# Token shift and the third head group's preparation in the merged projection stage, modulation in the chunk chain

## The chip, the core and the metric

The kernel runs on one core of a Trainium2 chip, as one launch. The metric is the device time of that launch in microseconds (us). TensorE, VectorE, ScalarE, GpSimd and SyncE run their own instruction streams and wait for each other on semaphores. In profile rows they are PE (with PEld for its weight loads), DVE, ACT, POOL and SP. All data is float32.

## The reference, cut to what matters

One diffusion step of a two-layer trunk over 640 tokens (128 of a prompt, 512 of a sample), width 1024. In each layer the modulated input h is multiplied by `w_in` into three groups of columns, each for one kind of token mixer: latent attention (8 heads), a gated linear recurrence "hgrn" (4 heads, two directions), and a delta-rule recurrence "rwkv" (4 heads, two directions), which is the third head group. Then follow an output projection with layernorm, an expert-choice layer and a second layernorm.

```python
cols = h @ p['w_in']
mla_cols, hg_cols, rw_cols = _split(cols, (MLA_COLS, HG_COLS, RW_COLS))
...
def _token_shift(a, mu):
    prev = jnp.pad(a[:, :-1], ((0, 0), (1, 0), (0, 0)))
    nxt = jnp.pad(a[:, 1:], ((0, 0), (0, 1), (0, 0)))
    return a + mu[0] * (prev - a) + mu[1] * (nxt - a)
...
feat = _token_shift(cols, mu)
r, k, v, wd_f, wd_b, ad_f, ad_b, gd = _split(feat, ...)
gate = jax.nn.sigmoid(gd) @ g2
kk = heads(k * k_k)
kk = kk * lax.rsqrt(jnp.maximum(jnp.sum(kk * kk, -1, keepdims=True), 1e-12))
for d, (wd, ad) in enumerate(((wd_f, ad_f), (wd_b, ad_b))):
    w_log = -jnp.exp(-jax.nn.softplus(-(w0[d] + jnp.tanh(wd) @ w2[d])) - 0.5)
    aa = jax.nn.sigmoid(a0[d] + ad @ a2[d])
    kd = heads(k * (1.0 + (aa - 1.0) * k_a))
    ... # recurrence over tokens, forward and backward
```

The modulation `silu(c) @ ada_w + ada_b` gives six vectors for each layer. Four of them (shift, scale and gates for what comes after the mixers) are needed only behind the mixers.

## The kernel before

Each layer is a row of phases, and a phase ends with a barrier of all engines. The phases that matter here are `phase_mix`, `phase_attention`, `phase_rwkv` and `phase_output`; the x tile, 5 x 1024 columns, is kept in its own memory, nearly everything else shares one arena.

**Merged projection stage (`phase_mix`).** h is transposed, and the projections are made in groups, each into one PSUM bank. A unit is one tile of 128 tokens in one direction of the hgrn recurrence, ten units in all, in an order written out by hand (`units`). For each unit TensorE makes the score products (`scores`, L712 and L722), a transposition (L739), one *item* of projection (`item`: two groups of eight matmuls), the output of the unit before (`out`, L755 to L769) and a state product (L779). The items are 5 of attention columns (m, lines L692 and L696), 2 of gates (g) and 9 of rwkv columns (r, both L684). Items alternate between banks 0 and 1; ScalarE evacuates each (`evacuate`, L850 for r). VectorE in each unit masks the scores (L1032), then makes half of the factors of a unit two ahead if the direction is forward (`run_levels`, 22 steps, L578 to L592) and the other half in the unit behind it (up to L611), then takes the output of the unit before (`collect`, L975 and L977) and updates the state (`state`, L994). GpSimd makes the factors of the backward units. After unit 9 come four more r items, the norm products of hgrn, and VectorE's reciprocals (L1059). rwkv columns lie in `rwT` with zero columns as padding.

**Attention (`phase_attention`).** 8 heads x 5 tiles of queries, software-pipelined over TensorE, VectorE and ScalarE. L1355 is the first rope operation of each head. Beside it GpSimd makes the token shift: for each of 9 rwkv chunks six scalings (L1318) and two additions (L1321, L1322). The x tile is loaded again here.

**rwkv (`phase_rwkv`).** First the preparation: tanh and squares on ScalarE (L1540, L1543), norm products (L1705), 16 low-rank products (`lora`, L1714), sigmoids out of them (L1552), reciprocals (L1906), the gate product (L1719), transpositions of v (L1726, L1729), then for each of four (direction, pair) a cumulative decay (L1920) with its exponentials and factors on VectorE, ScalarE and GpSimd (L1914 to L1937, L1573 to L1575, L1634 to L1646). Between these TensorE makes the four late vectors of the modulation (`modulate(s)`, L1691 and L1696) from 16 pieces of `ada_w`, 1 MB each, through four slots. L1965 is VectorE's first operation of the next part, in which 25 steps invert triangular blocks (L1758 to L1800). The last part is the chunk chain: ten steps, each with two chunks, that pass a state on: state products (L1839, L1844, twice), a copy by VectorE, a product with the inverse (L1861), the matrices of the next step (L1825, L1830), and the state update by VectorE (L2005, L2010). Normalisation and two rounds of transpositions end the phase (L1887).

**Output (`phase_output`).** The output projection (L2169) and the first layernorm, which reads the x tile.

## Time and profile before

| what | value |
|---|---|
| median of 3 runs | 3010.34 us (3006.26 to 3012.44) |
| the profiled execution's own time | 3006.61 us |
| its span, first to last instruction | 3004.8 us |
| PE busy | 2613.5 us (87%) |
| DVE, ACT, POOL busy | 1129.8, 467.5, 761.0 us |
| mean granted TensorE clock | 0.944 of full speed |

In a row, names are those of the program, L is the line, x is the number of instructions. A float32 matmul shows as two PE records. "Idle" is the time for which the engine stood still just before the row, with what ended it. The clock column gives the granted clock as a share of 2.4 GHz: 1.00 is the upper level, 0.50 the lower one, and what lies between is a mean over the stretch.

### The profile page before, as it was taken

Reading aid. Unit: us, or ns where it says so; the run is one execution under the profiler, and the core shown is the slowest. Engines: PE = TensorE matmul, PEld = TensorE weight load, DVE = VectorE, ACT = ScalarE, POOL = GpSimd, SP = SyncE. Lnnn points to the kernel's source line nnn. Section 1 sums busy time; section 2 is a strip of 40 time slices with the busy share of each in tenths; the row PEclk is TensorE's granted clock in tenths of the full one; section 3 lists DMA queues with packets and bytes.
Section 4 is the critical chain, followed back from the end, with each engine's and each line's share of the span. In section 5 each row is a group of like instructions: output and inputs, shape, how many; then the busy total and the mean of one; then the engine's idle time right before and its main releaser. Section 6 shows DMA issues by size and latency. Waiting matters only on the chain. (4 is left out here: it accounts for less than half of the span.)

```text
span 3004.8 us, 72192 instructions
## 1 busy us (share of the span) xinstructions
PE 2613.5 (87%) x32434; PEld 1773.8 (59%) x32434; DVE 1129.8 (38%) x2438; ACT 467.5 (16%) x992; POOL 761.0 (25%) x892
## 2 busy tenths in 40 slices
PE   6999888887675999999889997888977669999994
PEld 3677455467444666666446764553864456666662
DVE  3464356755433111111154724668453321111113
ACT  2100233421110000000031013334211100000001
POOL 1253092343041000000052522903421300000002
PEclk9999899999886999999999999999998789999997
DMA  7010200410345999999730102006005369999984
GB/s 282 15 38 29 76 1 1 182 53 30 120 166 189 387 398 387 397 396 402 293 138 16 43 22 76 1 1 232 4 29 212 141 235 395 395 397 390 398 351 140
DMA packets 76874, 560.56 MB, mean 187 GB/s; under 512 B 14056, under 2 KB 16168, under 8 KB 37656
## 3 DMA queue, kind: packets, MB, share of 16 engines
q1 hardware_dynamic: 70424, 534.97, 44.8%
q0 software_dynamic: 6144, 20.98, 3.1%
q8 instruction: 257, 4.21, 0.6%
q14 instruction: 49, 0.40, 0.0%
HBM read 528.78 MB, written 27.13 MB: 185 GB/s over the span
## 5 line engine op out<-in xcount | busy, mean ns | idle before, releaser
L2473 PEld LDWEIGHTS ps<-arena 128*64 128x64 f32 x16384 | 579.0, 138 | 89.7 <-issue 87.1
L2473 PE MATMUL ps<-arena 128*64 128x80 f32 x16384 | 599.4, 234 | 14.0 <-issue 9.4
L2487 PE MATMUL ps<-arena 128*80 128x512 f32 x1024 | 466.7, 600 | 0.0
L2548 DVE TENSOR_TENSOR arena<-arena,ps 128x160 f32<-128x160 f32 x128 | 41.1, 321 | 721.3 <-ACT arena L2508 721.3
L2487 PEld LDWEIGHTS ps<-arena 128*80 128x80 f32 x1024 | 143.7, 149 | 229.8 <-issue 218.9
L2508 ACT ACTIVATE arena<-ps 128x160 f32<-128x160 f32 x128 | 38.9, 304 | 1007.6 <-PE ps L2473 1007.6
L2234 POOL DMA_INDIRECT sum_d<-arena x32 | 45.6, 1427 | 583.6 <-DVE arena L2540 583.6
L2228 POOL DMA_INDIRECT arena<-h_d,arena x32 | 40.2, 1256 | 499.0 <-DVEq L2523 431.3
L684 PE MATMUL ps<-arena,x_sb 128*128 128x128 f32 (+1 forms) x576 | 158.5, 434 | 0.0
L684 PE MATMUL ps<-arena 128*128 128x512 f32 (+1 forms) x512 | 139.9, 434 | 4.5 <-ACT arena L833 4.5
L2169 PE MATMUL ps<-arena 128*128 128x512 f32 x320 | 141.9, 606 | 2.1 <-PEq L1502 2.1
L684 PEld LDWEIGHTS ps<-arena,x_sb 128*128 128x128 f32 x576 | 88.0, 191 | 69.1 <-issue 68.9
L684 PEld LDWEIGHTS ps<-arena 128*128 128x128 f32 x512 | 77.7, 191 | 65.3 <-issue 60.3
L2169 PEld LDWEIGHTS ps<-arena 128*128 128x128 f32 x320 | 62.0, 195 | 81.1 <-issue 81.1
L1364 DVE TENSOR_REDUCE arena<-ps 128x1 f32<-128x768 f32 (+1 forms) x80 | 65.8, 822 | 95.4 <-PE ps L1199 88.9
L1657 POOL TENSOR_TENSOR arena<-arena,rwl_sb 128x512 f32<-128x512 f32 x50 | 63.7, 1280 | 103.1 <-ACT arena L1587 56.2
L2540 DVE SCALAR_TENSOR_TENSOR arena<-ps,arena 80x512 f32<-80x512 f32 x64 | 45.0, 742 | 112.4 <-PE ps L2487 112.4
L1287 ACT ACTIVATE arena<-ps,arena 128x768 f32<-128x768 f32 (+1 forms) x80 | 63.6, 795 | 134.9 <-DVE arena L1365 112.8
L1032 DVE TENSOR_TENSOR arena<-ps,arena 128x512 f32<-128x512 f32 (+1 forms) x100 | 60.7, 634 | 61.8 <-PE ps L712 59.0
L1318 POOL TENSOR_SCALAR arena<-arena,pcol_sb 128x128 f32<-128x128 f32 x72 | 79.9, 1127 | 0.0
L1133 PE MATMUL ps<-arena 128*128 128x512 f32 (+1 forms) x192 | 59.0, 443 | 23.3 <-DVE arena L1355 23.3
L1212 PE MATMUL ps<-arena 128*64 128x64 f32 x1600 | 64.2, 226 | 16.0 <-DVE arena L1390 15.8
(352 smaller groups left out, 3856.8 us busy)
## 6 DMA issues: line engine op xcount, KB each, us to landing
arena<-in_ex_w SPq DMA_DIRECT2D x128, 2048.0 KB, 15.2
arena<-in_ex_w SPq DMA_DIRECT2D x128, 1024.0 KB, 13.4
arena<-in_ada_w SPq DMA_DIRECT2D x32, 1024.0 KB, 8.0
arena<-in_ada_w SPq DMA_DIRECT2D x8, 2048.0 KB, 16.3
x_sb<-in_w_t SPq DMA_DIRECT2D x18, 512.0 KB, 3.4
arena<-in_w_t SPq DMA_DIRECT2D x16, 512.0 KB, 6.2
x_sb<-in_x SPq DMA_DIRECT2D x2, 2560.0 KB, 18.3
h_d<-x_sb SPq DMA_DIRECT2D x10, 512.0 KB, 2.6
```

What stands on the lines that cost most here:

```text
L684: i = nc.tensor.matmul(dst[:, 0:c1 - c0], w[:, k, :], e.hT[:, k, c0:c1], start=k == 0, stop=k == KD - 1)
L1032: nc.vector.tensor_tensor(am[:, u % 2, at].rearrange("p (b n) -> p b n", b=rep), src.rearrange("p (b n) -> p b n", b=rep), hgf[:, dr:dr + ...
L1133: i = nc.tensor.matmul(ps[:, 7, 0:c1 - c0], uq[:, k, h * P:(h + 1) * P], cqT[:, k, c0:c1], start=k == 0, stop=k == 2)
L1212: m = nc.tensor.matmul(ps[c * C:(c + 1) * C, 6, (i % 2) * DV:(i % 2 + 1) * DV], pT[:, i % 2, k * P + c * C:k * P + (c + 1) * C], V[:, c0 / ...
L1287: nc.scalar.activation(pr[:, i % 2, 0:c1 - c0], sc[:, 0:c1 - c0], ACT.Exp, bias=negm[:, i:i + 1], scale=SCALE, accum_out=rsum[:, i:i + 1]) ...
L1318: c.add(nc.gpsimd.tensor_scalar(shifted[:, 1 + by, c0:c1], e.rwT[:, n, q0:q0 + c1 - c0], scale[:, n:n + 1], None, ALU.mult))
L1364: v.link(nc.vector.reduce_max(negm[:, i:i + 1], sc[:, 0:c1 - c0], AX))
L1657: nc.gpsimd.tensor_tensor(Mj[:, n % 4], raw[:, t], e.rwl[:, :, j + 2:j + 3, :].to_broadcast([P, 2, HH, C]), ALU.mult).then_inc(S["mj"], 1)
L2169: m = nc.tensor.matmul(ps[:, 2 * (t % 4) + n, :], e.mixT[:, k, t * P:(t + 1) * P], half, start=k == 0, stop=k == KD - 1)
L2234: e.nc.gpsimd.indirect_dma_start(e.sum_d, bass.IndirectOffsetOnAxis(ap=mem["iu"][:, x:x + 1], axis=0), mem["yR"][:, x % 2, :], None, compu ...
L2473: m = nc.tensor.matmul(gated(j)[c * 64:(c + 1) * 64, f, a, :], w13[q % WG][:, a, k, f * P + c * 64:f * P + (c + 1) * 64], xT[:, x % 2, k, ...
L2487: m = nc.tensor.matmul(rows_out(x, h), he[:, x % 2, f, :], w2[:, q % WP, f % 2, h * 512:(h + 1) * 512], start=f == 0, stop=f == KD - 1)
```

## The change

- **Token shift.** Each r item is evacuated by ScalarE with the scale 1 - mu0 - mu1 (`om`), and VectorE then adds mu0 times the token before and mu1 times the token after straight from the item's PSUM bank: four operations (`shift`). The bank is free only after the last of them. The padding and the GpSimd work in attention go.
- **Order of the items.** g and r items come first, the five m items last, behind unit 9. r items follow in the order 6, 7, 2, 3, 0, 1, 8, 4, 5. All their weights go through a ring of five slots in the x tile.
- **Preparation.** Tanh, squares, norm products (two new items n, each two matmuls with an evacuation by VectorE), square roots and the reciprocals (`norms`) are made in units 3 to 9. Behind unit 9 come the 16 `lora` products through four banks, then the m items; beside these run the sigmoids, decays, exponentials and factors (`lora_out`, `exponents`, `keys`, `scaled`, `decays`, `factors`). Their results stay in memory through attention: `KB` at the arena's end, `AR` in the x tile.
- **Modulation.** `modulate(i)` handles one piece, and two pieces are put in each step of the chunk chain: one behind the first round of state products, one at the step's end. The slots are three.
- **Loads.** The x tile is loaded again after the last step of the chunk chain. The first half of `w_out` is loaded behind the last piece of `ada_w`. Attention's weights lie elsewhere. `phase_mix` has more semaphores, which SyncE clears at the start of attention.

The diff, cut to its core:

```diff
@@ phase_mix: the items and their banks
-    groups += [("m", t, s) for t in range(TILES) for s in range(2)]
-    groups += [("g", c, s) for c in range(2) for s in (1, 0)]
-    groups += [("r", c, s) for c in range(NRW) for s in (1, 0)]
+    gates, shifts_a, shifts_b, shifts_c = (0, 1), (6, 7, 2, 3, 0), (1,), (8, 4, 5)
+    items = [("g", c) for c in gates] + [("r", c) for c in shifts_a] + [("n", p) for p in range(2)]
+    items += [("r", c) for c in shifts_b + shifts_c] + [("m", t) for t in range(TILES)]
...
+    served = [[("g", 0)], [("g", 1), ("r", 6)], [("r", 7)], [("r", 2)], [("r", 3)], [("r", 0)],
+              [("n", 0), ("n", 1), ("r", 1)], [("r", 8)], [("r", 4)], [("r", 5)]]
...
-        return n % 8 if n < NX else n % 2
+        return n % 8 if n < NX else n % 2 if kind != "m" else ((0, 1), (6, 7), (0, 1), (2, 3), (4, 5))[a][s]
@@ phase_mix, TensorE
             for u in range(1, U):
                 scores(u)
                 if units[u] not in last:
                     turn(u)
-                item(u + (u > 1))
+                for i in served[u][:1] if u == 1 else served[u]:
+                    item(*i)
                 out(u - 1)
                 if units[u] not in last:
                     chunk_state(u)
                 if u == 1:
-                    item(2)
-            item(11)
+                    item(*served[u][1])
             out(U - 1)
-            item(12)
-            item(13)
+            for n, (w, dr, pair, i) in enumerate(lora):
+                if n >= 4:
+                    pe.wait_ge(S["lo_ev"], n - 3)
+                nc.tensor.matmul(ps[:, lora_bank[n % 4], 0:c1 - c0], wwa[...], F[:, 6 + w, c0:c1], ...)
+            item("m", 0)
             ...
@@ phase_mix, VectorE
+            def shift(kind, c):
+                ...
+                dve.wait_ge(S["rw_om"], 2 * k + 2)
+                for i in range(2):
+                    v.add(nc.vector.scalar_tensor_tensor(F[:, c, c0 + 1:c1], ps[...], col("mu0", c), F[:, c, c0 + 1:c1], ALU.mult, ALU.add))
+                v.join()
+                for i in range(2):
+                    nc.vector.scalar_tensor_tensor(F[:, c, c0:c1 - 1], ps[...], col("mu1", c), ...).then_inc(S["pj_dve"], 1)
...
+                if u in (7, 8):
+                    norms(u - 7)
...
                 if dr == 0 and u + 2 < U:
                     nxt = run_levels(u + 2)
                     ...
+                for kind, i in served[u]:
+                    if kind != "g":
+                        shift(kind, i)
                 if u:
                     collect(u - 1)
@@ phase_attention
-            sp.dma_start(e.x[:, :, :], (e.x_d if l else d["x"])...).then_inc(S["ld_xr"], 16)
...
-            for n in range(NRW):
-                for by, scale in ((0, om), (-1, mu[0]), (1, mu[1])):
-                    ...
@@ phase_rwkv, TensorE
                 with_state(2, chunks, 0, s, S["rh_ps"])
+                if 0 <= 2 * s - 1 < ADA_PIECES:
+                    modulate(2 * s - 1)
                 pe.wait_ge(S["rh_sb"], s + 1)
...
                 with_state(3, chunks, 1, s, S["y_ps"])
+                if 2 * s < ADA_PIECES:
+                    modulate(2 * s)
@@ phase_rwkv, SyncE
             sp.wait_ge(S["rw_fin"], 1)
+            sp.wait_ge(S["y_ps"], 2 * NS)
+            sp.dma_start(e.x[:, :, :], (e.x_d if l else d["x"])...).then_inc(S["ld_xr"], 16)
```

## Rows read from the trace of the kernel before

**Rows 1.** Stretches: width, busy us (instructions) of PE, PEld, DVE, ACT, POOL, clock, DMA:

```profile
40.80:338.70 297.90, 293.98 (x1904) 200.97 (x1904) 148.93 (x370) 47.29 (x91) 107.93 (x236) 0.99 0.13 47
338.70:545.00 206.30, 171.51 (x1390) 105.57 (x1390) 113.14 (x253) 68.39 (x162) 88.43 (x75) 0.95 0.08 29
545.00:616.50 71.50, 58.48 (x245) 21.07 (x245) 56.48 (x64) 34.48 (x60) 25.08 (x16) 0.90 0.63 243
616.50:706.00 89.50, 78.77 (x2580) 76.75 (x2580) 45.24 (x75) 19.17 (x38) 41.78 (x36) 0.94 0.04 9
706.00:803.60 97.60, 61.35 (x915) 54.49 (x915) 56.31 (x106) 17.18 (x37) 21.79 (x28) 0.86 0.05 20
2027.00:2095.40 68.40, 55.70 (x244) 20.02 (x244) 56.47 (x64) 34.22 (x59) 25.09 (x16) 0.95 0.66 254
```

**Rows 2.** Timeline, units 6 and 7: start, duration, engine, line [idle before]:

```profile
228.76 8.82 PE L684 MATMUL ps<-arena,x_sb 128*128 128x512 f32 x32
...
237.04 0.29 DVE L584 TENSOR_TENSOR arena<-arena 128x128 f32<-128x128 f32 x1
...
240.67 0.42 DVE L977 COPY arena<-ps 128x256 f32<-128x256 f32 x1 [3.33 <-PE ps L769]
...
242.43 1.97 DVE L1032 TENSOR_TENSOR arena<-ps,arena 128x512 f32<-128x512 f32 x3 [0.21 <-DVE arena L994]
...
254.87 0.42 DVE L611 TENSOR_TENSOR arena<-arena 128x256 f32<-128x256 f32 x1
...
256.98 0.42 DVE L975 TENSOR_TENSOR arena<-arena,ps 128x256 f32<-128x256 f32 x1 [1.68 <-PE ps L769]
```

**Rows 3.** Groups by line, whole span: busy us, mean ns of one:

```profile
L1059 DVE RECIPROCAL arena<-arena 128x640 f32<-128x640 f32 x4 | 16.6, 4153 | 34.8 <-ACT arena L908 34.8
```

**Rows 4.** Attention: line L1318 (ns, first and last start), and timeline of VectorE:

```profile
L1318 POOL TENSOR_SCALAR arena<-arena,pcol_sb x36: 599/1336/1809, 380.1 to 462.1; 128x128 f32<-128x128 f32 x18, 128x512 f32<-128x512 f32 x18
...
408.75 0.70 DVE L1355 TENSOR_TENSOR arena<-ps,rope_sb 32x512 f32<-32x512 f32 x1
...
429.22 0.70 DVE L1355 TENSOR_TENSOR arena<-ps,rope_sb 32x512 f32<-32x512 f32 x1
...
511.04 0.70 DVE L1355 TENSOR_TENSOR arena<-ps,rope_sb 32x512 f32<-32x512 f32 x1
```

**Rows 5.** Timeline, rwkv preparation:

```profile
566.48 2.40 PE L1719 MATMUL ps<-arena 128*128 128x256 f32 x10 [2.72 <-ACT arena L1554]
...
573.92 1.22 ACT L1561 ACTIVATE arena<-ps 128x1280 f32<-128x1280 f32 x1
...
591.26 3.25 PE L1738 MATMUL ps<-blk_sb,arena 128*128 128x2 f32 x20
...
618.68 0.75 DVE L1965 TENSOR_TENSOR arena<-ps,rwl_sb 128x256 f32<-128x256 f32 x2 [0.50 <-PE ps L1758]
```

**Rows 6.** Timeline of TensorE: one modulation piece, and waits in the chunk chain:

```profile
586.00 1.89 PE L1691 MATMUL ps<-arena,scT 128*2 128x512 f32 x8 [0.61 <-DMA arena<-in_ada_w]
...
733.82 0.70 PE L1839 MATMUL ps<-arena 128*64 128x128 f32 x4 [4.49 <-DVEq L2016]
...
754.06 0.68 PE L1861 MATMUL ps<-arena 64*64 64x64 f32 x16 [0.55 <-DVE arena L2001]
...
759.79 0.44 PE L1839 MATMUL ps<-arena 128*64 128x128 f32 x4 [1.42 <-DVEq L2016]
```

**Rows 7.** Timeline, state update beside and without GpSimd's constants:

```profile
727.93 2.91 POOL L1678 TENSOR_TENSOR arena<-arena 128x1280 f32<-128x1280 f32 x1
...
729.49 4.22 DVE L2010 TENSOR_TENSOR arena<-arena 128x256 f32<-128x256 f32 x2 [0.47 <-PE ps L1844]
...
751.12 1.16 DVE L2010 TENSOR_TENSOR arena<-arena 128x256 f32<-128x256 f32 x2 [0.48 <-PE ps L1844]
```

**Rows 8.** Timeline, end of the rwkv phase:

```profile
800.23 2.39 PE L1887 MATMUL ps<-ident_sb,arena 128*128 128x128 f32 x10 [12.50 <-DVEq L2042]
```

**Rows 9.** DMA issues: count, KB each, median us to landing:

```profile
x_sb<-in_x SPq DMA_DIRECT2D x2, 2560.0 KB, 18.3
```

More of the change, by code:

```diff
@@ L53 @@
 SCALE = float(QK) ** -0.5
-PAD = NTOK + 3
 TOKC = MLA_COLS + HH * HD
@@ L634, in _, with ring_load @@
             sp.wait_ge(S["pj_ps"], NX)
-            sp.dma_start(w_m1, d["w_m1"][l]).then_inc(S["ld_m1"], 16)
-            sp.dma_start(w_m2a, d["w_m2"][l, :, 0:6]).then_inc(S["ld_m2"], 16)
-            sp.wait_ge(S["pj_ps"], NH)
-            for c in range(2):
-                sp.dma_start(gw[c], d["w_t"][l, HGT + c]).then_inc(S[f"ld_gw{c}"], 16)
+            def ring_load(i):
+                kind, c = ring[i]
+                if i >= WRING:
+                    sp.wait_ge(S["pj_ps"], begins[ring[i - WRING]] + 2)
+                slot, _, w = weights(kind, c)
+                sp.dma_start(w, d["w_t"][l, HGT + c + 2 * (kind == "r")]).then_inc(S[f"ld_wt{slot}"], 16)
+            for i in range(WRING + 2):
+                ring_load(i)
             sp.wait_ge(S["hg_state"], 2)
@@ L658, in project @@
                 kind, a, s = groups[n]
-                if n < NX:
-                    if n >= 8:
-                        evacuated(pe, n - 8)
-                elif n == NX:
+                before = [m for m in range(n) if pbank(m) == pbank(n)]
+                if before:
+                    evacuated(pe, before[-1])
+                if n == NX:
                     for m in range(NX - 2, NX):
                         evacuated(pe, m)
-                elif n > NX + 1:
-                    evacuated(pe, n - 2)
                 dst = ps[:, pbank(n), :]
@@ L795, in _ @@
                 evacuated(pe, m)
-            item(0)
+            for i in served[0]:
+                item(*i)
             for u in range(1, U):
@@ L892, in _ @@
                 evacuate(n)
-            item(0)
+            for i in served[0]:
+                item(*i)
             for u in range(1, U):
@@ L909, in _ @@
                                      bias=e.eps[:, 0:1], scale=1.0 / HD).then_inc(S["hg_rt"], 1)
-            item(14)
-            item(15)
+            exponents(2)
+            item("m", 1)
+            exponents(3)
+            for t in range(2, TILES):
+                item("m", t)
             e.done("act", a)
@@ L1437, in phase_rwkv @@
     So, z1 = e.part(z1, 4, P)
-    assert z1 <= e.a1
+    assert z1 <= e.a0 + 2560
     X, z1 = e.part(e.a1, TILES, 2, HH, C)
-    assert z1 <= e.a1 + 4 * PAD
+    assert z1 <= e.a1 + 4 * NTOK
     ys, z1 = e.part(e.a1, TILES, HH * HD)
-    assert z1 <= e.a1 + 4 * PAD
-    ada = [e.part(late + n * 2048, 2, 2, 512)[0] for n in range(ADA_SLOTS)]
-    assert late + ADA_SLOTS * 2048 <= z
-    above = e.a2 + 4 * NCH * 2 * C + 4 * 2 * NTOK
+    assert z1 <= e.a1 + 4 * NTOK
+    ada = []
+    for _ in range(ADA_SLOTS):
+        v, z = e.part(z, 2, 2, 512); ada.append(v)
+    above = e.a2
     arow = e.part(above, 4, 512)[0]
     abias = e.part(above + 4 * 512, 512)[0]
-    mid, z = e.part(z, 4, NCH)
-    end, z = e.part(z, 4, NCH)
-    G, z = e.part(z, 4, NCH)
     Gb, z = e.part(z, 4, NCH, 2)
@@ L1518, in _ @@
                              ).then_inc(S[f"ld_ap{i % ADA_SLOTS}"], 16)
+            sp.wait_ge(S["ap_ps"], ADA_PIECES)
+            k = 0
+            for dst in first_half(e):
+                n = dst.shape[1]
+                sp.dma_start(dst, d["w_out"][l, :, 0, k:k + n, :]).then_inc(S["ld_wo0"], 16)
+                k += n
             sp.wait_ge(S["ap_row"], 8)
@@ L1716, in _, with modulate @@
-            pe.wait_ge(S["lo_ev"], len(lora))
-            pe.wait_ge(S["rw_sg"], 1)
+            def modulate(i):
+                s = i // 4
+                if i == 0:
+                    pe.wait_ge(S["ld_ab"], 16)
+                if i % 4 == 0 and s >= 2:
+                    pe.wait_ge(S["ap_row"], 2 * (s - 1))
+                pe.wait_ge(S[f"ld_ap{i % ADA_SLOTS}"], 16 * (i // ADA_SLOTS + 1))
+                for k in range(2):
+                    for c in range(2):
+                        m = nc.tensor.matmul(gate_sums(s)[c], e.scT[:, 2 * (i % 4) + k, :], ada[i % ADA_SLOTS][:, c, k, :],
+                                             start=i % 4 == 0 and k == 0, stop=False, skip_group_check=True)
+                m.then_inc(S["ap_ps"], 1)
+                if i % 4 == 3:
+                    for c in range(2):
+                        r = C + 2 * s + c
+                        m = nc.tensor.matmul(gate_sums(s)[c], e.ident[C:C + 8, r:r + 1].to_broadcast([8, 2]), abias[C:C + 8],
+                                             start=False, stop=True, skip_group_check=True)
+                    m.then_inc(S["ap_sum"], 1)
```

506 lines of the change are left out of this document (263 added, 243 removed).

## The prediction

> **What bounds the kernel now.** I read the table of stretches first, since the change moves work between stages with different limits. In layer 0 the merged stage takes 297.90 us and TensorE is busy for 293.98 of them, at a granted clock of 0.99: TensorE sets its pace. In attention no engine is near full (TensorE 171.51 of 206.30 us), and GpSimd's 88.43 us lie beside the others. In the preparation of rwkv (71.50 us) TensorE has 58.48, VectorE 56.48, ScalarE 34.48; chains of products and elementwise work set it, and the clock is 0.90. The inverse takes 89.50 us at 0.94, the chunk chain with its tail 97.60 at 0.86 with TensorE busy for 61.35 [rows 1]. Then I read the timeline where the new work is to go. The collections of units 6 and 7 begin 16.3 us apart (240.67 and 256.98), and in unit 6, whose item starts at 228.76, VectorE, done with its factor steps at 237.33, stands idle 3.33 us before it collects; in unit 7 it ends its factors at 255.29 and stands idle 1.68 [rows 2]. So an even unit has some 3.3 us of room on VectorE and an odd one some 1.7 or less.
>
> The profiled execution took 3006.61 us, 1.8 more than its span, and 3.7 less than the median of 3010.34. I make the sum as a difference and put it on the median.
>
> **Merged stage.** A shift is four operations of VectorE that read PSUM, two of 512 columns and two of 128. The nearest row is a 512-column operation with PSUM input at 0.70 us [rows 4]; with 0.35 for the narrow ones, which is my choice (half; no row has it), that is 2.1 us. Bounds are 1.4 (overlapped) and 4.2 (double). A shift delays the collection behind it, and with it the state and the next mask.
> - Units 2, 4, 8, 9 have 3.3 us of room: 0.
> - Units 3 and 5 have about 1.5: +0.6 each, +1.2.
> - Unit 1 has two items, and the second one's ring slot and shift stand behind the state product: shift, collection, state and mask take 2.1, 0.4, 0.9 and 2.0 us (the mask 1.97 [rows 2]), 5.4 in all, against 2.4 of work of TensorE beside them: +3.0.
> - Unit 6 has both norm products and item r1. Only two banks alternate, so the second norm product needs the first one's bank evacuated by VectorE, which has issued its 22 factor steps ahead of it. These end at 237.33 [rows 2]. Then 0.7 of evacuation, the product, and again an evacuation before r1: r1 starts at 240.0 instead of 228.76. That is +11.2.
> - In unit 7 `norms` puts a reciprocal of 4.15 us [rows 3] ahead of the factor steps, and a shift of 2.1 behind them, of which 1.68 is room; with 0.5 for the multiplication, +5.1. Unit 8 has the same reciprocal but even unit's room and no factor steps of the same length: 0.
> - The 16 `lora` products behind unit 9 take 8 pairs of 1.10 (8.82/8, the rate of an item [rows 2]) = 8.8 if nothing holds them, and 13.2 if ScalarE's sigmoids, through four banks, set the pace. I take 10.9. The m items that follow give cover for all that VectorE, ScalarE and GpSimd still do: TensorE has about 10.9 + 9.6 + 2.8 + 4 x 9.6 = 61.7 us there, VectorE about 46, GpSimd 41 to 53. So the tail costs 0 with 9 to 15 us of room.
> - Clock. Where TensorE has stood still for long, the rows behind show it slow: the same state product takes 0.70 us after 4.49 of idle, 0.44 otherwise [rows 6]. The stage has 0.99 now. I expect the 8.3 us of idle in unit 6 to bring such a stretch of some 7 us, 3.6 lost, and as much in sum in the other places: +7.0; bounds 0 and 14.
>
> Sum: 1.2 + 3.0 + 11.2 + 5.1 + 10.9 + 7.0 = +38.4 per layer.
>
> **Attention.** GpSimd's scalings run from 380.1 to 462.1; a head that has them beside it takes 20.47 us (408.75 to 429.22), and the next four (429.22 to 511.04), two of them without, 20.46 each [rows 4]. Taking them away gives 0. Sixteen more semaphores are cleared by SyncE before the loads: +0.7.
>
> By the Trainium skill, "SBUF — State Buffer", section "SBUF: two separate sides", GpSimd and VectorE hold a shared pair of ports one at a time, so that without GpSimd's scalings VectorE should run freer; the head's 20.47 and 20.46 us do not agree that it costs time here, and the sum would be lower by what the heads gained.
>
> **Preparation.** Now 73.7 us from 545.00 [rows 1] to L1965 at 618.68 [rows 5]. What stays: start and loads that land 3.9 us in, the gate product with the transpositions and the last evacuation (566.48 to 573.92 + 1.22 = 8.7 [rows 5]), at the lower clock some 4.5 more, the bonus product (3.25 at 591.26 [rows 5]; I take 2.8), 3.3 of last copies and the start 0.5: 23.7. That is -50.0. In layer 1 the stage is 68.40 long, 3 less [rows 1]: -47.1. Bounds: 17 and 31 us remaining.
>
> **Modulation in the chain.** A chain step is set by the state's way through TensorE and VectorE. A piece behind the first state products takes 1.89 [rows 6] and lies where TensorE waits 0.55 for VectorE's copy [rows 6]; 1.34 is added to the path, 8 times, 10.7. A piece at the step's end lies beside a wait of 1.42 [rows 6]: 0.5 added, 6 times (two are covered otherwise), 3.0. Four bias rows at 0.5: 2.0. The slow clock of the chain (0.86 [rows 1]) is partly won back by a busier TensorE, -3.7. Together +12. Bounds +2 (all in gaps that rows show larger at the start, 4.49 [rows 6]) and +24 (all 16 pieces on the path with their bias rows). The weights' ring of three slots is a DMA of 1 MB per step and has time: 0.
>
> **Loads.** The x tile is issued when the last y product is done, about 787.2, and first read behind the wait of 12.50 us for the normalisation, which ends at 800.23 [rows 8]; the load of 2560 KB took 18.3 us median to landing [rows 9], beside attention's weights. Alone I estimate 10 us and so 0; at 18.3 it would cost 4.8 per layer. `w_out` and the other moved loads have 2 to 3 us of room at least: 0, and 3 if not.
>
> **Sum.** Layer 0: 38.4 + 0.7 - 50.0 + 12 = +1.1. Layer 1: 38.4 + 0.7 - 47.1 + 12 = +4.0. Both: +5.1, and 3010.3 + 5.1 = 3015.4; I say 3015.5.
>
> **Rivals.**
> *A, the forecast:* the moved work costs on TensorE's path what it saved. Its own range 3004 to 3027. Chance 0.40.
> *B, the clock (the other side):* a stage of 0.90, one of 0.94 and one of 0.86 [rows 1] lie behind one another. If the 0.99 of the merged stage stays in spite of unit 6, and the shorter preparation and the fuller chain let the clock stay up, the 7.0 of loss go, and of the 4.7 + 8.6 us that the low clock costs the inverse and the chain now (78.77 x 0.06 and 61.35 x 0.14) I let half, 6.7, come back: 13.7 per layer, minus 27 in all, near 2988. It decides for faster from 5.6 us per layer. For it: TensorE loses many of its waits. Against it: unit 6's stall is as long as the ones behind which rows show it slow. Chance 0.25.
> *C, the shift on VectorE:* the 2.1 us (4.2 at the upper bound) come through in every unit, because VectorE's room exists in no unit once its steps are late, and the clock does not recover before unit 8: 8 x 0.7 more of shift and 5.5 of clock, +11 per layer, near 3038. For it: VectorE has 148.93 us busy in the stage [rows 1], in bursts before TensorE's waits. Chance 0.20.
> *D, GpSimd and VectorE in the tail:* the state update took 4.22 us beside GpSimd's 2.91 us addition, and 1.16 without it [rows 7]. If the two engines' 35 to 47 and 41 us behind unit 9 go one after the other, they need 76 to 88 against 61.7 of TensorE: +14 per layer at the lower end, near 3043. Against it: most of VectorE's operations there are narrow or have PSUM or one input, and 88.43 us of GpSimd slowed no head in attention [rows 1, 4]. Chance 0.08.
>
> The exclusive lock of the Trainium skill, "SBUF — State Buffer", section "SBUF: two separate sides", is the reason why this could go so for operations with two SBUF inputs; on the state update the trace agrees with it.
>
> *E, the x load:* it lands late, +4.8 per layer, near 3025. Chance 0.07.
>
> **How the numbers follow.** About 0.2% (6 us) is what a measurement of this kernel can tell from no change. Faster means below 3004.3: nearly all of B (0.24) and 0.07 of A, 0.31. Same, up to 3016.4: about 0.19 of A, the rest of B and 0.02 of E, 0.22. Slower: 0.14 of A, C, D and the rest of E, 0.47. A range that leaves out 2 in 10 goes from under B's 2988 to over D's 3043: 2984 to 3046, as the cases have both signs.
>
> **What would show it.** In the merged stage an idle of over 7 us of TensorE ahead of r1 in unit 6, and one of 4 to 5 in unit 7; a stage longer by 35 to 42 us; heads of 20.5 us; L1965 some 23 us into the rwkv phase; chain steps that grow by 1.3 to 1.8 us where they hold pieces; no wait for the x tile. Wrong it would be if unit 6's stall were short, if the granted clock of inverse and chain rose to 0.98 or more, or if VectorE's row of the tail ended behind the last m item.

## The result: 0.6% faster, where no change was forecast

The changed kernel takes 2991.65 us (median of 5 runs, 2987.45 upward), the kernel before 3009.07 in the same measurement; the ratio is 0.994, with a 95% interval of 0.9924 to 0.9956. The forecast was 3015.5, a little over no change. The time lies in the range, 2984 to 3046, but on the other side of the kernel before than the forecast did, 24 us from it. One of the five runs took 3296 us and was disturbed; the median of the other four is 2990.2 us, and the ratio leaves it out.

The profiled execution of the changed kernel has a span of 2989.5 us against 3004.8. Both spans can be divided at the same operations: the first projection, attention's first transposition, the first product of the inverse, the first matrix product of the chunk chain, the transposition of its final state, the first product of the output projection. Differences of such starts, in us:

| stretch | layer 0 before | after | difference | layer 1 before | after | difference |
|---|---|---|---|---|---|---|
| first projection to attention | 295.91 | 324.77 | +28.86 | 295.91 | 325.09 | +29.18 |
| attention and rwkv preparation | 270.36 | 221.32 | -49.04 | 267.03 | 219.91 | -47.12 |
| inverse | 87.10 | 87.34 | +0.24 | 87.86 | 90.59 | +2.73 |
| chunk chain | 83.28 | 92.48 | +9.20 | 81.33 | 92.50 | +11.17 |
| tail up to the output projection | 16.79 | 16.79 | 0.00 | 16.86 | 16.80 | -0.06 |

With the 0.71 us ahead of the first projection and -0.50 and -0.6 behind the output projections these make -15.3. The forecast had +39.1, -50.0 (-47.1), 0 and +12 for them. Three of the four are right to a few us. The first is 10 us too high in each layer, 20 of the 24 us of the miss.

Here are the stretches of the changed kernel in layer 0, as in [rows 1]: the last m items with all the elementwise work beside them, what is left of the preparation, the inverse, the chain.

```profile
318.50:366.10 47.60, 47.56 (x170) 27.22 (x168) 42.58 (x30) 19.00 (x32) 39.20 (x22) 1.00 0.00 1
577.10:597.00 19.90, 12.53 (x60) 10.48 (x60) 1.94 (x8) 5.41 (x13) 0.00 (x0) 0.74 0.48 173
597.00:684.40 87.40, 76.91 (x2562) 75.21 (x2562) 44.26 (x71) 18.56 (x37) 42.64 (x36) 0.94 0.02 4
684.40:776.90 92.50, 86.42 (x1065) 53.26 (x1065) 45.73 (x97) 17.17 (x38) 22.83 (x28) 1.00 0.50 172
```

The preparation is 19.90 us long where it was 71.50 [rows 1]. The chain has become a stretch of TensorE, 86.42 of 92.50 us at the upper level of the clock. The row of [rows 1] for the chain, with its 0.86, also holds the wait for the normalisation at its end. Between the same two operations as in the last row above, the kernel before had 0.92:

```profile
703.60:786.90 83.30, 59.87 (x921) 53.35 (x921) 46.51 (x97) 12.48 (x30) 21.79 (x28) 0.92 0.07 27
```

 In the first row of the changed kernel TensorE has no gap at all: what VectorE, ScalarE and GpSimd do there is hidden.

The timeline of the changed kernel's TensorE, and two rows of VectorE, through units 6 to 8 and behind unit 9:

```profile
229.16 1.25 PE L731 MATMUL ps<-arena,blk_sb 128*128 128x512 f32 x4
...
237.91 2.50 PE L731 MATMUL ps<-arena,blk_sb 128*128 128x512 f32 x4 [7.50 <-DVE arena L1152]
...
240.76 9.41 PE L727 MATMUL ps<-arena,x_sb 128*128 128x512 f32 x32 [0.36 <-DVE arena L1152]
...
271.22 0.70 PE L769 MATMUL ps<-arena 128*128 128x256 f32 x2 [1.48 <-DVEq L1112]
...
275.72 1.60 PE L759 MATMUL ps<-arena 128*128 128x128 f32 x12 [1.58 <-DVE arena L1236]
...
307.98 7.02 PE L864 MATMUL ps<-arena 128*128 128x512 f32 x24
...
316.26 2.43 PE L864 MATMUL ps<-arena 128*128 128x512 f32 x8 [1.26 <-ACT arena L958]
```

```profile
237.17 0.88 DVE L1152 TENSOR_SCALAR arena<-ps 128x512 f32<-128x512 f32 x2
...
258.14 4.14 DVE L1170 RECIPROCAL arena<-arena 128x640 f32<-128x640 f32 x1
```

The stall of unit 6 is where it was forecast: TensorE stands for 7.50 us until VectorE, behind its factor steps, evacuates the first norm products at 237.17. The item behind it starts at 240.76, forecast 240.0. But it runs in 9.41 us, nearly the 8.82 of [rows 2]. The clock is at its lower level for 6.8 us, from 235.0 to 241.8, and TensorE is at work in only 3.53 of them: the rest is stall (columns as in [rows 1]).

```profile
233.00:234.00 1.00, 0.00 (x0) 0.00 (x0) 0.96 (x4) 0.00 (x0) 0.84 (x3) 1.00 0.00 0
235.00:241.80 6.80, 3.53 (x6) 1.69 (x7) 3.81 (x13) 0.00 (x0) 0.23 (x1) 0.50 0.01 2
242.00:243.00 1.00, 1.00 (x3) 0.38 (x2) 0.00 (x0) 0.00 (x0) 0.00 (x0) 1.00 0.00 0
```

The intervals between the starts of two units' score products, read from the same timelines (us; layer 1 agrees to 0.05 except where noted):

| unit | 0 | 1 | 2 | 3 | 4 | 5 | 6 | 7 | 8 |
|---|---|---|---|---|---|---|---|---|---|
| before | 28.71 | 24.94 | 15.80 | 16.70 | 16.30 | 16.31 | 16.31 | 16.30 | 15.86 |
| after | 28.27 | 24.17 | 17.10 | 16.31 | 16.31 | 16.30 | 28.51 | 17.86 | 17.70 |

An m item takes some 0.4 us longer than an r or g item, so the units that lost m items (0, 1 with two, 2 and 3) are shorter by that, and the tail behind unit 9 longer. In unit 2 the interval grew by 1.3 us in spite of it; the wait there is 1.7.

### The profile page after: what moved, and what is told of

The parts are those of the page before. It is cut to its first block and busy times, and to the rows that moved or that the text cites. A ratio compares the mean times of both kernels' runs of the same rounds, so it can differ in the third digit from the quotient of the medians.

```text
span 2989.5 us, 72116 instructions
## 1 busy us (share of the span) xinstructions
PE 2615.2 (87%) x32434; PEld 1776.5 (59%) x32434; DVE 1151.2 (39%) x2486; ACT 477.8 (16%) x1000; POOL 614.1 (21%) x754
## 5 line engine op out<-in xcount | busy, mean ns | idle before, releaser
L2549 PEld LDWEIGHTS ps<-arena 128*64 128x64 f32 x16384 | 579.7, 138 | 87.0 <-issue 84.3
L2549 PE MATMUL ps<-arena 128*64 128x80 f32 x16384 | 600.2, 234 | 11.2 <-issue 6.6
L727 PE MATMUL ps<-arena,x_sb 128*128 128x512 f32 (+1 forms) x704 | 195.5, 436 | 2.3 <-ACT arena L916 1.6
L727 PEld LDWEIGHTS ps<-arena,x_sb 128*128 128x128 f32 x704 | 108.4, 192 | 88.5 <-issue 84.7
L2245 PEld LDWEIGHTS ps<-arena 128*128 128x128 f32 x320 | 62.6, 196 | 81.6 <-issue 81.4
L727 PE MATMUL ps<-arena 128*128 128x128 f32 (+1 forms) x384 | 104.6, 434 | 4.3 <-DVE arena L1213 4.3
L727 PEld LDWEIGHTS ps<-arena 128*128 128x128 f32 x384 | 58.1, 191 | 49.8 <-issue 45.0
L1359 PE MATMUL ps<-arena 128*128 128x512 f32 (+1 forms) x192 | 59.6, 447 | 23.4 <-DVE arena L1565 23.4
L1438 PEld LDWEIGHTS ps<-arena 128*64 128x64 f32 x1600 | 53.3, 138 | 41.1 <-DVE arena L1600 26.4
L1422 PE MATMUL ps<-arena 96*128 96x512 f32 (+1 forms) x160 | 74.6, 547 | 2.5 <-ACT arena L1500 2.5
```

The costliest lines, as they stand in the source:

```text
L727: i = nc.tensor.matmul(dst[:, 0:c1 - c0], w[:, k, :], e.hT[:, k, c0:c1], start=k == 0, stop=k == KD - 1)
L1359: i = nc.tensor.matmul(ps[:, 7, 0:c1 - c0], uq[:, k, h * P:(h + 1) * P], cqT[:, k, c0:c1], start=k == 0, stop=k == 2)
L1422: m = nc.tensor.matmul(ps[:, 2 * (i % 2), 0:min(512, c1 - c0)], QT[:, h % 2, t * P:(t + 1) * P], Kh[:, h % 2, c0:min(c0 + 512, c1)], start ...
L1438: m = nc.tensor.matmul(ps[c * C:(c + 1) * C, 6, (i % 2) * DV:(i % 2 + 1) * DV], pT[:, i % 2, k * P + c * C:k * P + (c + 1) * C], V[:, c0 / ...
L2245: m = nc.tensor.matmul(ps[:, 2 * (t % 4) + n, :], e.mixT[:, k, t * P:(t + 1) * P], half, start=k == 0, stop=k == KD - 1)
L2549: m = nc.tensor.matmul(gated(j)[c * 64:(c + 1) * 64, f, a, :], w13[q % WG][:, a, k, f * P + c * 64:f * P + (c + 1) * 64], xT[:, x % 2, k, ...
```

## The experiments

All twelve kernels are edits of the changed kernel; 3, 8 and 12 join several. Each was timed beside the kernel before, whose median lay between 3007.5 and 3009.4 us. Differences below are against the changed kernel's 2991.65. Its own interval is 0.9924 to 0.9956, and those of 2, 4, 7 and 11 overlap it; what these four show rests on the intervals of units, which repeat to some 0.01 us, and not on their medians.

**1. The norm products evacuated first.** In VectorE's loop over units:

```diff
+                for kind, i in served[u]:
+                    if kind == "n":
+                        shift(kind, i)
                 if dr == 0 and u + 2 < U:
                     nxt = run_levels(u + 2)
...
-                    if kind != "g":
+                    if kind == "r":
                         shift(kind, i)
```

> Unit 6: VectorE evacuates the two norm products ahead of its 22 factor steps instead of behind them. Theory 1 (the stall is VectorE's order, and the lower clock behind it is small): the waits of 7.50 and 0.36 us go, and with them the 1.25 + 0.59 us by which the second norm products and the item behind the stall ran slower; 9 to 10 us per layer, 18 to 20 in all, some 2973 us. Theory 2 (the forecast's clock term of 7.0 us per layer is real and hangs on this stall): 14 us per layer and more, under 2965. Theory 3 (the stall only moves, to the factor steps that come 3 us later): less than 4 us per layer, over 2984.

Measured: 2970.13 us, ratio 0.9871 (0.9856 to 0.9887), 21.5 us less. TensorE in unit 6:

```profile
229.17 1.25 PE L731 MATMUL ps<-arena,blk_sb 128*128 128x512 f32 x4
...
230.98 1.35 PE L731 MATMUL ps<-arena,blk_sb 128*128 128x512 f32 x4 [0.56 <-DVE arena L1152]
```

The wait of 7.50 is one of 0.56 and the unit takes 20.12 us in both layers instead of 28.5: 8.4 each, 16.8 in all. Theory 1 stands for the stall. The remaining 4.7 us of the medians are not in any unit; where the profiled executions differ besides is told below.

**2. Both reciprocals in unit 8.**

```diff
-                if u in (7, 8):
-                    norms(u - 7)
+                if u == 8:
+                    for p in range(2):
+                        norms(p)
```

> Both reciprocals (4.14 us each) in unit 8, where VectorE has no factor steps, instead of one in unit 7 and one in unit 8. Theory 1 (in unit 7 the reciprocal delays the factors that unit 8's scores wait for): unit 7 goes from 17.86 to 16.3 us and unit 8 from 17.70 to 15.9, 3.4 per layer, 6.8 in all, some 2985 us. Theory 2 (the two together push unit 8's shift and collection): the gain of unit 7 comes back as a wait in unit 8, within 2 us of 2991.6.

Measured: 2984.71 us, ratio 0.9916 (0.9899 to 0.9933), 6.9 less. Unit 7 takes 16.31 us and unit 8 15.85, in both layers: theory 1, to the tenth. Unit 8's scores wait for unit 8's factors, and these stood behind the reciprocal in unit 7; in unit 8 there are no factors left to make. The wait for the masks in unit 8 goes too, with the token shift as wide as before.

**3. Both edits together.**

> The edits of the two kernels before together. If both waits are independent: 26 us in all less than the changed kernel, some 2965 to 2967 us, with TensorE's granted clock at 1.00 through units 2 to 9. If VectorE's lateness is one and the same in units 6 to 8: no more than the first edit alone, some 2973.

Measured: 2964.76 us, ratio 0.9852 (0.9837 to 0.9866), 26.9 less. The two waits are independent. Units 6, 7 and 8 take 20.13, 16.30 and 15.86 us. The same stretch of unit 6, first in the changed kernel, then in this one:

```profile
224.80:253.40 28.60, 20.74 (x156) 14.10 (x151) 15.40 (x42) 3.99 (x5) 9.19 (x21) 0.88 0.00 1
```

```profile
222.90:243.10 20.20, 19.07 (x160) 13.43 (x157) 14.71 (x42) 2.93 (x6) 10.93 (x26) 1.00 0.00 1
```

TensorE is busy for 20.74 and 19.07 us: the lower clock made its work 1.7 us longer, no more, though the mean clock of the stretch was 0.88.

**4. A narrow token shift.** Both additions of a shift work on 8 columns of each block:

```diff
-   v.add(nc.vector.scalar_tensor_tensor(F[:, c, c0 + 1:c1], ps[:, pbank(n + i), 0:c1 - c0 - 1], col("mu0", c), ...))
+   v.add(nc.vector.scalar_tensor_tensor(F[:, c, c0 + 1:c0 + 9], ps[:, pbank(n + i), 0:8], col("mu0", c), ...))
...
-   nc.vector.scalar_tensor_tensor(F[:, c, c0:c1 - 1], ps[:, pbank(n + i), 1:c1 - c0], col("mu1", c), ...)
+   nc.vector.scalar_tensor_tensor(F[:, c, c0:c0 + 8], ps[:, pbank(n + i), 1:9], col("mu1", c), ...)
```

> The token shift works on 8 columns of each block only (the rest is left out), with the same four instructions and semaphores. Theory 1 (VectorE's room covers the shift nearly everywhere): the waits of 1.43 us in unit 2 and 1.58 in unit 8 go, about 3 us per layer, 6 in all, some 2985 us. The forecast's terms for it (3.0 + 1.2 + 1.7 per layer): 12 in all, 2980. The rival in which the shift comes through in every unit (2.1 us each, nine units, two layers): 30 and more, under 2962.

Measured: 2986.6 us, ratio 0.9925 (0.9908 to 0.9941), 5.1 less. Unit 2 takes 15.81 us (17.10) and unit 8 16.41 (17.70): 2.6 us per layer, 5.2 in all. Units 3 to 5 and 7 are as they were. The shift costs nothing there; its width costs 1.3 us in each of two units. In unit 8 that holds only as long as the reciprocal stands in unit 7: kernel 2 has the whole shift and no wait there, so the two gains don't add.

**5. A double token shift.** The four operations are issued twice, with the item's bank given back after the last (each neighbour is then added twice).

> The token shift's four operations are issued twice (each neighbour is added twice), 2.1 us more of VectorE behind each rwkv item, with the item's bank held longer. Theory 1 (even units have 3.3 us of room and the shift uses 2.1 of it, odd units less): the waits come out at 1 to 2 us in most units, 6 to 12 us per layer, 12 to 24 in all, 3004 to 3016 us. The rival of no room anywhere: 2.1 x 9 x 2 = 38 us, 3029. Full cover: 0.

Measured: 3022.53 us, ratio 1.0041 (1.0029 to 1.0053), 30.9 more, above what theory 1 gave and below the 38 of the rival. The units 2 to 8 take 20.87, 18.26, 18.21, 17.47, 29.74, 19.02, 21.44 us: 3.8, 2.0, 1.9, 1.2, 1.2, 1.2 and 3.7 more, 14.9 in sum per layer. In units 3 and 4 TensorE waits in the middle of the scores for VectorE's masks:

```profile
184.38 1.60 PE L759 MATMUL ps<-arena 128*128 128x128 f32 x12 [1.68 <-DVE arena L1246]
...
202.60 1.60 PE L759 MATMUL ps<-arena 128*128 128x128 f32 x12 [1.64 <-DVE arena L1246]
```

So the cover is real but thin: in units 3 to 7 the first shift is free (kernel 4), and of the 2.0 us of the second more than half is paid, in even and odd units alike. Units 2 and 8 grow by more than the work that was added; the items behind their waits take 10.20 and 9.51 us instead of 8.82, so part of it is the clock. The rival without any room, 38 us, is near for the second shift and wrong for the first.

**6. Thin modulation in the chain.** Each piece multiplies 32 of 512 columns (the others are left out); loads, waits and the bias rows stay.

```diff
-   m = nc.tensor.matmul(gate_sums(s)[c], ..., ada[i % ADA_SLOTS][:, c, k, :], ...)
+   m = nc.tensor.matmul(gate_sums(s)[c][:, 0:32], ..., ada[i % ADA_SLOTS][:, c, k, 0:32], ...)
```

> The modulation's pieces in the chain work on 32 of 512 columns (the other columns are left out), with the same loads and waits; the bias rows stay. Theory 1 (TensorE is now the chain's limit, so that the pieces cost what does not fit in the 1.97 us of waits of a step): the chain goes from 92.5 us back to 83 to 85, 16 to 19 in all, some 2974 us. Theory 2 (the fuller chain wins back clock, 3.7 us per layer as forecast): the chain without pieces falls to a clock of 0.92 to 0.94 and takes 86 to 88, 9 to 13 in all, some 2981 us.

Measured: 2975.05 us, ratio 0.9887 (0.9865 to 0.9908), 16.6 less. The chain takes 85.49 and 85.23 us, 7.1 less per layer, 14.3 in all. Its stretches in the two layers:

```profile
682.50:768.00 85.50, 69.09 (x1065) 57.22 (x1065) 44.28 (x97) 17.17 (x38) 22.80 (x28) 0.90 0.53 186
2147.10:2232.30 85.20, 67.37 (x1064) 56.53 (x1064) 45.79 (x97) 17.17 (x38) 22.81 (x28) 0.92 0.54 187
```

Without the full pieces the clock falls from 1.00 to 0.90 and 0.92, as theory 2 says (it gave 0.92 to 0.94) and theory 1 leaves out. The length of the chain lies between the two, and the time, 2975, is the one that theory 1 gave. The full pieces bring some 17 to 18 us of TensorE's time into the chain (86.4 less 69.1, and 85.5 less 67.4), and the chain gets 7 longer. The two parts of that can be seen in the sums by line over the chain of layer 0, for the kernel before, the changed kernel and this one (busy us, mean ns, idle us before with what ended it). First the state products, the product with the inverse and the matrices before the change:

```profile
L1839 PE MATMUL ps<-arena 128*64 128x128 f32 x160 | 17.4, 297 | 17.2 <-DVEq L2016 16.1 <-DVE arena L1995 1.0
...
L1825 PE MATMUL ps<-arena 64*128 64x128 f32 x160 | 13.4, 313 | 0.9 <-DVE arena L1980 0.9
...
L1861 PE MATMUL ps<-arena 64*64 64x64 f32 x160 | 7.7, 242 | 5.5 <-DVE arena L2001 5.5
```

The same and the pieces and bias rows in the changed kernel:

```profile
L1835 PE MATMUL ps<-arena,scT 128*2 128x512 f32 x128 | 30.2, 592 | 0.0
L1960 PE MATMUL ps<-arena,x_sb 128*64 128x128 f32 x160 | 16.6, 286 | 4.2 <-DVEq L2092 3.2 <-DVE arena L2071 1.0
...
L1946 PE MATMUL ps<-x_sb,arena 64*128 64x128 f32 x160 | 11.6, 284 | 0.9 <-DVE arena L2057 0.9
...
L1984 PE MATMUL ps<-arena 64*64 64x64 f32 x160 | 6.8, 224 | 1.1 <-DVE arena L2077 1.1
...
L1841 PE MATMUL ps<-arena,ident_sb 8*2 8x512 f32 x16 | 4.1, 586 | 0.0
```

And two of them with thin pieces:

```profile
L1960 PE MATMUL ps<-arena,x_sb 128*64 128x128 f32 x160 | 16.6, 286 | 13.2 <-DVEq L2092 12.2 <-DVE arena L2071 1.0
...
L1946 PE MATMUL ps<-x_sb,arena 64*128 64x128 f32 x160 | 15.3, 346 | 0.9 <-DVE arena L2057 0.9
```

The pieces fill 17.3 us of waits (16.1 to 3.2, and 5.5 to 1.1), and the matrices, the same products, take 11.6 us instead of 13.4, or of 15.3 with thin pieces.

**7. TensorE busy in unit 6's stall.** The second product of the first norm item is issued 13 times.

```diff
+                    for _ in range(13 if (a, s) == (0, 0) else 1):
                         i = nc.tensor.matmul(dst[:, 0:c1 - c0], e.blk[:, :], rn[:, a, c0:c1], start=True, stop=True)
```

> The second product of the first norm item is issued 13 times instead of once (its result is the same), so that TensorE is at work through most of the 7.50 us for which it stood in unit 6; VectorE's order stays that of the changed kernel. If the low clock behind the stall costs the 1.84 us that the rows behind it show (2.50 against 1.25, 9.41 against 8.82): unit 6 goes from 28.5 to some 26.7 us, 2 to 4 us in all, some 2988 us. If the forecast's clock term were right (3.6 us behind this stall, 7.0 per layer): 24.9 us or less, 7 to 14 in all, 2978 to 2985.

Measured: 2988.9 us, ratio 0.9935 (0.9922 to 0.9949); not to be told from the changed kernel. The repeated products took less time than I had given them and left a wait of 4.81 us, behind which TensorE was slow again (10.65 us for the item in layer 0). Unit 6 took 29.73 and 28.28 us, the first longer than in the changed kernel. The clock was at its lower level for 6.8 us again, but it fell at the end of the shorter stall, and TensorE was at work in nearly all of them:

```profile
236.40:243.20 6.80, 5.96 (x8) 2.68 (x9) 1.52 (x4) 0.00 (x0) 0.00 (x0) 0.50 0.00 0
```

A wait that is only shortened need not give the clock back, and kernel 11 fills all of it.

**8. One norm item a unit.** Norm items behind the r items of units 6 and 7, both reciprocals in unit 8, square roots at the end of unit 7.

```diff
-              [("n", 0), ("n", 1), ("r", 1)], [("r", 8)], [("r", 4)], [("r", 5)]]
+              [("r", 1), ("n", 0)], [("r", 8), ("n", 1)], [("r", 4)], [("r", 5)]]
```

> One norm item behind the rwkv item of unit 6, the other behind that of unit 7, and both reciprocals in unit 8; nothing then waits for an evacuation of norm products. Against the kernel with both orders changed (unit 6 20.12 us): unit 6 and 7 each 16.3 + 0.7 us, so 2.4 us per layer less, some 2960 us. If the square roots come too late for the reciprocals in unit 8: unit 8 grows from 15.9 by what unit 6 gives back, 2965.

Measured: 2977.17 us, ratio 0.9891 (0.9876 to 0.9906): faster than the changed kernel but 12 us slower than 3. Both branches of what I expected were wrong. Units 6 and 7 take 21.45 and 23.48 us, unit 8 15.85.

```profile
240.60 1.51 PE L731 MATMUL ps<-arena,blk_sb 128*128 128x512 f32 x4 [2.29 <-DVE arena L1164]
...
262.80 2.50 PE L731 MATMUL ps<-arena,blk_sb 128*128 128x512 f32 x4 [3.04 <-DVE arena L1164]
```

The norm product needs the bank that the r item before it holds, and that is free only when the shift (L1164) is done. In unit 7 the shift stands behind the factor steps. In unit 6 these end 1.2 us before it, and it waits for ScalarE's evacuation of the item; the 2.29 us there are the item's way through ScalarE and VectorE, not VectorE's order. I had looked at who waits for the norm products and not at what they wait for.

**9. Both pieces of a step together.**

```diff
-                if 0 <= 2 * s - 1 < ADA_PIECES:
-                    modulate(2 * s - 1)
+                for i in (2 * s, 2 * s + 1):
+                    if i < ADA_PIECES:
+                        modulate(i)
...
-                if 2 * s < ADA_PIECES:
-                    modulate(2 * s)
```

> Both modulation pieces of a chain step behind its first state products, none at its end. Theory 1 (each piece hides in the wait beside it, 0.55 us there and 1.42 at the end): the end's wait comes back in the eight steps, 1.0 to 1.4 us each, 8 to 11 us per layer, 16 to 22 in all, some 3010 us. Theory 2 (TensorE is full, so the place does not matter): within 3 us of 2991.6.

Measured: 3010.03 us, ratio 1.0007 (0.9995 to 1.0019), 18.4 more: the whole gain of the change goes. The chain takes 103.52 and 105.06 us. The wait at the end of a step is back at the size of [rows 6]:

```profile
741.22 0.44 PE L1960 MATMUL ps<-arena,x_sb 128*64 128x128 f32 x4 [1.42 <-DVEq L2091]
...
752.49 0.44 PE L1960 MATMUL ps<-arena,x_sb 128*64 128x128 f32 x4 [1.42 <-DVEq L2091]
```

Theory 1. In the changed kernel the piece at a step's end fills that wait; eight times 1.42 is 11.4 us, and the chain grew by 11.0 and 12.6.

**10. The modulation ahead of the inverse.** All 16 pieces behind the bonus product, and the wait for their sums there; `w_out` is still loaded in the chain's eighth step, and ScalarE reads the four vectors out ahead of the inverse too (not shown).

```diff
             pe.wait_ge(S["bo_ev"], 1)
+            for i in range(ADA_PIECES):
+                modulate(i)
+            pe.wait_ge(S["ap_row"], 8)
...
-                if 0 <= 2 * s - 1 < ADA_PIECES:
-                    modulate(2 * s - 1)
...
-                if 2 * s < ADA_PIECES:
-                    modulate(2 * s)
```

> All 16 modulation pieces back ahead of the inverse, behind the bonus product (the load of the output weights stays where it is in the chain). Theory 1 (16 MB through three slots set this stretch; what hid them before was the preparation that is gone): some 8 us lie behind the start of the loads, the rest of 48 to 62 us of transfer is waited for; the preparation grows from 19.9 to 60 to 75 us, the chain shrinks from 92.5 to 81 to 83; 30 to 45 us per layer more, 3050 to 3080 us. Theory 2 (the pieces cost their 1.89 us each wherever they are): 30 - 10 = 20 per layer, 3032.

Measured: 3071.85 us, ratio 1.0198 (1.0181 to 1.0216), 80.2 more. The preparation is as long as before the change:

```profile
577.80:650.60 72.80, 49.52 (x208) 15.58 (x208) 1.93 (x8) 10.14 (x21) 0.00 (x0) 0.87 0.64 235
```

```profile
606.31 1.88 PE L1836 MATMUL ps<-arena,scT 128*2 128x512 f32 x8 [1.71 <-DMA arena<-in_ada_w]
...
619.69 1.89 PE L1836 MATMUL ps<-arena,scT 128*2 128x512 f32 x8 [2.85 <-DMA arena<-in_ada_w]
```

The pieces wait for their weights. The transfer of 16 MB sets this stretch, and VectorE, 56.48 us busy in [rows 1], has 1.93 us to do in it. But the transfer also stands still for some 12 us, from 590 to 602, because the three slots are full until the pieces in them are used behind the bonus product:

```profile
590.00:599.50 9.50, 6.86 (x35) 4.85 (x35) 0.00 (x0) 3.39 (x8) 0.00 (x0) 0.72 0.02 6
```

In the kernel before, with four slots and pieces from 573.05 on, two loads of work lay side by side there, the elementwise work and the transfer. With this placement and three slots, moving the elementwise work alone gains nothing, and the 50 us come only when the transfer has gone too. What a placement that fills the 12 us would gain, no run shows. The chain is 84.02 us with this edit, 8.5 less.

**11. The stall filled.** As 7, with 31 issues.

> As the filled stall before, with 31 issues of the norm product instead of 13, since those covered only 2.7 of the 7.50 us and 4.81 us of standing still were left. If the clock behind the stall is what the rows show (some 1.3 to 3.4 us between executions): unit 6 goes to some 26.7 us, 2 to 6 us in all, 2986 to 2989 us. If the forecast's term of 7.0 us per layer hung on it: 2978.

Measured: 2985.31 us, ratio 0.9926 (0.9911 to 0.9941), 6.3 less.

```profile
229.30 7.95 PE L732 MATMUL ps<-arena,blk_sb 128*128 128x512 f32 x64
...
238.02 1.35 PE L732 MATMUL ps<-arena,blk_sb 128*128 128x512 f32 x4 [0.78 <-DVE arena L1153]
```

Unit 6 takes 27.04 and 27.03 us, against 28.51 and 28.54: the clock behind the stall costs 1.5 us there, 3 of the 6.3 us (2.7 per layer against an execution in which the unit took 29.73). The second norm product takes 1.35 us where it took 2.50.

**12. The shift of chunk 6 earlier.** Kernel 3, with the items of unit 1 in the order r6, g1.

> Both orders changed, and in unit 1 the rwkv item comes ahead of the gate item, so that its token shift lies in VectorE's 10.7 us of idle time and not ahead of unit 2's masks. If the wait of 1.43 us in unit 2 is the shift's: unit 2 goes from 17.1 to 15.8 us, 2.6 us in all less than the kernel with both orders, some 2962 us. If the wait is the mask's own: no change.

Measured: 2963.35 us, ratio 0.9848 (0.9835 to 0.9862), within the uncertainty of 3. Unit 2 takes 15.42 us (17.10), unit 1 24.80 (24.17): 1.05 per layer less. With 3 it is the fastest of all, 1.5% under the kernel before.

## Why the prediction was wrong

**The step that failed is the sum of the merged stage: "1.2 + 3.0 + 11.2 + 5.1 + 10.9 + 7.0 = +38.4 per layer", with 0.7 for attention's start. It measured 28.9 and 29.2.** Term by term:

| term | forecast | measured | from |
|---|---|---|---|
| unit 1, second item and shift | 3.0 | 1.7, in unit 2 | 17.10 less 15.42, kernel 12; 1.3 by kernel 4 |
| units 3 and 5 | 1.2 | 0 | intervals 16.31, 16.30 |
| unit 6, order of VectorE | 11.2 | 12.2, 1.5 of it the clock | interval 28.51 less 16.31, kernel 11 |
| unit 7 (and 8) | 5.1 | 3.4, half of it in unit 8 | kernel 2 |
| low-rank products | 10.9 | 10.6 | 307.98 to 318.53 |
| clock after stalls | 7.0 | 1.5, counted in unit 6 | kernel 11 |
| start of attention | 0.7 | 1.2 | idle 9.66 against 8.46 |

The third row holds the clock of the sixth. The mechanisms were there, with the named engine; only that of unit 1 lies elsewhere, in the mask of unit 2. Four sizes of the sum were off, all upward. The largest is the clock term, 5.5 of the 10 us.

**Clock.** I took "some 7 us, 3.6 lost" behind unit 6's stall from a stretch in which TensorE had idled for 4.49 us [rows 6], and as much again for the other places. The stretch came, 6.8 us long, but half of it lay in the stall itself. Only 1.5 us are lost between the profiled executions of the changed kernel and kernel 11, and nothing in the other places: the items of the units 1 to 5 and 7 to 9 take 8.82 to 8.92 us each. The 0.88 that kernel 3's first row shows for unit 6 is a mean over a stretch in which TensorE stood still for over a quarter of the time, and a low clock costs nothing then. What counts is the length of the matmuls behind the stall. Rival B, near 2988, came out as the number but not as it was argued. Its first half is right, the loss in the merged stage is small. Its second half is wrong for the inverse, which has 0.94 as before and takes no less time (+0.24, +2.73). For the chain it is right that the clock rose, to 1.00, past the 0.98 that the prediction names as a sign of being wrong; but the chain did not get shorter than forecast by the 4.3 us that B wanted, only by 2.8 and 0.8. Both B and the forecast took the chain's 0.86 from a row with the tail in it; the chain itself had 0.92 in layer 0.

**Shift.** The room of VectorE was read from the rows in even units (3.33 us) and held. In units 3 and 5 I had charged 0.6 and there was enough too. In unit 1, where I had charged 3.0 to the collection behind the shift, the shift waits for its item while VectorE stands idle; what is delayed is the mask of unit 2. The wait of 1.7 us goes when the shift is moved into that idle time (kernel 12, which pays 0.6 of it back in unit 1). Kernel 5 shows how little was left: rival C, in which 2.1 us come through in every unit, describes the second shift and not the first. Without the token shift's additions the changed kernel would gain 5 us, half of which kernel 2 gets without leaving them out.

**Unit 7.** The reciprocal does delay factors, by 4.14 us, and the scores of unit 8 wait 1.48 for them and 1.58 for the masks; the remaining 1.1 us of it cost nothing.

**What was right.** The preparation: attention and preparation together lost 49.0 and 47.1 us, forecast 50.0 and 47.1; the preparation of layer 0 alone lost 51.6, and the slow heads of attention (below) took some back. The chain: +9.2 and +11.2, forecast +12, by pieces in the waits beside them (kernel 9) and a clock that comes back (kernel 6). That the sum came so close is in part luck. The bias rows take 4.1 us, forecast 2.0, and the chain's other products take 68.4 us where they took 73.8, 5.4 less, forecast 3.7 (layer 0, six lines of products, three of them shown with kernel 6); the two misses largely cancel. The x tile, the weights' ring and `w_out` cost nothing; the wait for the normalisation is the one of [rows 8] again, and the output projection starts 3.44 us behind it as before:

```profile
790.20 2.39 PE L2013 MATMUL ps<-ident_sb,arena 128*128 128x128 f32 x10 [12.50 <-DVEq L2118]
```

**GpSimd's work in attention** was worth nothing, as forecast: most heads take 20.44 us (20.46). But in the profiled execution of the changed kernel two heads were longer:

```profile
416.90:438.80 21.90, 19.70 (x163) 12.25 (x163) 12.62 (x28) 6.69 (x15) 0.00 (x0) 0.92 0.00 1
438.80:460.90 22.10, 19.84 (x163) 12.41 (x163) 12.55 (x28) 6.36 (x15) 0.00 (x0) 0.92 0.00 1
460.90:481.40 20.50, 18.17 (x163) 11.44 (x163) 12.59 (x30) 6.43 (x15) 0.00 (x0) 1.00 0.01 2
```

Their work is the same and TensorE's clock is 0.92. In the other kernels such a dip comes in one layer, in both or in neither, costs 1.5 to 3.2 us, and falls on the second or third head. Why it comes is open; no run here was made to tell. In the profiled executions it costs the changed kernel 4.8 us in the two layers, and kernels 1, 6 and 11 3.2, 1.6 and 0. That is of the size of the 4.7, 2.3 and 3.4 us that their medians gained beyond the units or the chain, but it does not split them: other stretches differ by 1 to 4 us as well, among them the chain, 96.1 instead of 92.5 us in one layer of kernels 3 and 4.

**Rival D** is closer than its chance of 0.08 says. Behind unit 9 VectorE has 42.58 us and GpSimd 39.20 in a stretch of 47.60 (the first row of stretches above), and they do slow each other. An operation of VectorE with GpSimd at work beside it, one of the same shape alone, and VectorE's wait at the end:

```profile
342.98 1.54 POOL L1069 TENSOR_TENSOR x_sb<-x_sb,arena 128x640 f32<-128x640 f32 x1
343.16 2.04 DVE L1188 TENSOR_TENSOR arena<-arena 128x640 f32<-128x640 f32 x1
...
344.70 1.90 POOL L1068 TENSOR_TENSOR arena<-arena 128x640 f32<-128x640 f32 x1 [0.18 <-POOL x_sb L1069]
...
361.25 0.82 DVE L1200 TENSOR_TENSOR x_sb<-x_sb,arena 128x640 f32<-128x640 f32 x1
...
366.09 1.56 DVE L1291 TENSOR_TENSOR arena<-arena 128x640 f32<-128x640 f32 x2 [4.03 <-PE ps L743]
```

VectorE's operation spans 2.04 us against 0.82, and ends 0.68 us behind GpSimd's; GpSimd's next, begun while VectorE's still ran, ends 1.40 us behind that. That is one after the other. The Trainium skill says it so in "SBUF — State Buffer", section "SBUF: two separate sides": the shared pair is "an exclusive lock, not a bandwidth split", taken by VectorE for operations with two SBUF inputs against GpSimd's that read SBUF. The trace agrees for these operations. It does not decide the stage, because much of VectorE's time there takes no such lock (8.33 us are two reciprocals with GpSimd beside them, each as long as in the kernel before, [rows 3], where GpSimd had nothing to do beside them); VectorE's last factors end at 362.07, TensorE's last item at 366.06. The room is 4 us and not the 9 to 15 of the forecast; 3.6 of the difference is TensorE's own work, 58.1 us behind unit 9 and not 61.7.

## What to carry to other kernels

A low mean clock over a stretch with a stall in it says little of what the clock costs. Only the part in which TensorE works counts: compare the lengths of the same matmuls behind the stall, or keep TensorE busy through it, before you put a clock term in a sum. When a small operation is put into an in-order engine's program, its place decides: the same two evacuations cost 8.4 us a layer more behind 22 steps than ahead of them, and it has to be asked both who waits for the operation and what it must wait for itself. When two kinds of work fill a stage side by side, here 16 MB of weights and the elementwise preparation, moving the one gained nothing (with the placement of kernel 10) until the other went too, and the second has to be placed where waits of its size are: one piece into each wait, not two into one.
